# Laying the preparation of a unit out to end one step sooner in each round of a chunked recurrence

## What is computed

```python
def step(S, inp):
    r_t, w_t, k_t, v_t, kk_t, a_t = inp
    sa = jnp.einsum("bhvk,bhk->bhv", S, kk_t)
    S = (S * w_t[:, :, None, :]
         - sa[..., None] * (kk_t * a_t)[:, :, None, :]
         + v_t[..., None] * k_t[:, :, None, :])
    return S, jnp.einsum("bhvk,bhk->bhv", S, r_t)

def rwkv7_readout(o, streams, r_k, gn_g, gn_b, w_out, out_dtype):
    r, v, _, _, _, kd, g = streams
    mean = jnp.mean(o, axis=-1, keepdims=True)
    var = jnp.mean(jnp.square(o - mean), axis=-1, keepdims=True)
    y = ((o - mean) * lax.rsqrt(var + GN_EPS)).reshape(B, T, RW_WIDTH) * gn_g + gn_b
    ...
```

## Time and profile before

| what | value |
|---|---|
| median of 3 runs | 2528.25 us (2522.92 to 2529.23) |
| the profiled execution, its own time | 2539.45 us |
| its span, first to last instruction | 2537.7 us |
| granted TensorE clock, mean | 0.939 of full speed |
| rounds 0 to 20 of the recurrence in it | 562.6 to 1161.4 us, 598.8 us |

### The profile page before, as it was taken

One profiled execution on the slowest core, in us unless ns is written; L12 is line 12 of the kernel. 1 busy time (PEld: TensorE's weight loads), 2 busy tenths in 40 slices (PEclk: granted clock), 3 DMA queues, 4 the chain that ended last, 5 costly groups with the idle time before them and its releaser, 6 DMA issues.

```text
span 2537.7 us, 59405 instructions
## 1 busy us (share of the span) xinstructions
PE 2172.6 (86%) x25764; PEld 1625.2 (64%) x25764; DVE 1354.0 (53%) x2324; ACT 1152.3 (45%) x1933; POOL 681.8 (27%) x412
## 2 busy tenths in 40 slices
PE   8799999288888888887789999996888987898888
PEld 2587777067766767676667666663666665666666
DVE  1357878434444455454345666664356663466752
ACT  2466767233333334343335454543355553355552
POOL 0334443200001011011433222222443332433332
PEclk9899999589998899998989999997999998999998
DMA  7215453652332222312313111111222221222222
GB/s 259 71 59 170 132 159 117 179 147 78 100 105 75 68 63 51 78 43 71 135 56 108 51 50 54 55 42 43 90 75 83 67 67 66 67 79 76 63 67 67
DMA packets 156163, 221.37 MB, mean 87 GB/s; under 512 B 84480, under 2 KB 109312, under 8 KB 155136
## 3 DMA queue, kind: packets, MB, share of 16 engines
q1 hardware_dynamic: 144800, 174.32, 22.4%
q0 software_dynamic: 9952, 40.11, 5.2%
q10 hardware_dynamic: 1152, 3.15, 0.3%
HBM read 164.84 MB, written 42.21 MB: 82 GB/s over the span
## 4 chain that ended last, share of the span: by engine, by line
PE 59%; DVE 15%; ACT 11%; issue 8%; POOL 4%; DMA 2%; SPq 0%; ACTq 0%; DVEq 0%; POOLq 0%
PE ps L257 8%; PE ps L259 7%; PE ps L258 7%; PE ps L1337 3%; PE ps L543 3%; PE ps L1327 2%; PE ps L1352 2%; PE ps L2257 2%; PE ps L396 2%; PE ps L2794 2%; PE ps L2217 1%; PE ps L2771 1%; PE ps L1202 1%; ACT p L2277 1%; DVE s L921 1%
## 5 line engine op out<-in xcount | busy, mean ns | idle before, releaser
L242 POOL TENSOR_TENSOR wbl<-wb,wbh 128x1024 fp32r<-128x1024 f32 x128 | 309.4, 2418 | 661.3 <-ACT wbh L237 657.5
L257 PE MATMUL ps<-hTh,wah 128*128 128x512 f32 (+1 forms) x512 | 180.6, 353 | 17.3 <-POOL wal L242 10.8
L257 PE MATMUL ps<-hT2h,wbh 128*128 128x512 f32 x416 | 180.2, 433 | 10.7 <-POOL wbl L242 10.5
L258 PE MATMUL ps<-hTl,wah 128*128 128x512 f32 (+1 forms) x512 | 174.9, 342 | 0.0
L259 PE MATMUL ps<-hTh,wal 128*128 128x512 f32 (+1 forms) x512 | 174.7, 341 | 0.0
L257 PE MATMUL ps<-hT1h,wbh 128*128 128x512 f32 (+1 forms) x432 | 169.0, 391 | 3.1 <-POOL hT1l L2398 3.1
L344 POOL TENSOR_TENSOR ro<-ro 128x256 f32<-128x256 f32 (+1 forms) x12 | 11.9, 993 | 586.7 <-DVE ro L328 586.7
L237 ACT ACTIVATE wbh<-wb 128x1024 fp32r<-128x1024 f32 x128 | 134.6, 1052 | 69.5 <-PE ps L1936 43.5
L259 PE MATMUL ps<-hT2h,wbl 128*128 128x512 f32 x416 | 164.5, 395 | 0.0
L258 PE MATMUL ps<-hT2l,wbh 128*128 128x512 f32 x416 | 163.9, 394 | 0.0
L242 POOL TENSOR_TENSOR wal<-wa,wah 128x1024 fp32r<-128x1024 f32 x34 | 102.2, 3008 | 219.2 <-ACT wah L237 219.2
(11 more groups left out here) (410 smaller groups left out, 5612.6 us busy)
## 6 DMA issues: line engine op xcount, KB each, us to landing
wb<-in_w_in SPq DMA_DIRECT2D x56, 512.0 KB, 3.5
s_str_dram<-s POOLq DMA_DIRECT2D x48, 576.0 KB, 8.7
wm<-in_ada SPq DMA_DIRECT2D x48, 512.0 KB, 4.5
bkv<-s_str_dram SPq DMA_DIRECT2D x96, 192.0 KB, 3.3
wa<-in_rw_in SPq DMA_DIRECT2D x34, 512.0 KB, 4.4
wb<-in_da_in SPq DMA_DIRECT2D x32, 512.0 KB, 3.4
ARI<-s_str_dram SPq DMA_DIRECT2D x96, 128.0 KB, 3.4
wb<-in_w_out SPq DMA_DIRECT2D x16, 512.0 KB, 3.5
```

The source lines that it names most:

```text
L242: e.tensor_tensor(self.lo[:, n % 2], self.raw[:, n % 3], self.hi[:, n % 2].bitcast(F32), ALU.subtract).then_inc(self.K.s.w_lo, 1)
L257: e.matmul(z, wh[:, k, :], hi[:, k, a:b], start=k == 0, stop=False)
L258: e.matmul(z, wh[:, k, :], lo[:, k, a:b], start=False, stop=False)
```

## The change

The number that `pace` gets for the preparation goes from 7 to 8, and from 11 to 12 in a round with a readout. The generators have seven and eleven steps as before, so the preparation's steps fall due at 1/8, 2/8, ... instead of 1/7, 2/7, ..., with nothing due at the end.

```diff
             if u + 3 < 24:
-                parts.append((prepared(u + 3), 11 if self.read_with(u + 3) else 7))
+
+                parts.append((prepared(u + 3), 12 if self.read_with(u + 3) else 8))
             pace(*parts)
```

## The result

| | before | after |
|---|---|---|
| median | 2528.74 us (2522.92 to 2531.06, 4 runs) | 2557.59 us (2547.14 to 2562.4, 4 runs) |
| ratio | 1 | 1.0104, interval 1.0083 to 1.0126 |
| the profiled execution | 2539.45 us | 2547.14 us |
| its span | 2537.7 us | 2545.3 us |
| its mean granted clock | 0.939 | 0.946 |

The medians are 28.9 us apart. The ratio, which is not the quotient of the two medians, says 1.0%, or 26 us (21 to 32). The forecast was 32.1 us slower and 2560 us.

What follows compares the result with a forecast made beforehand. PE bounds the kernel; its 89 us idle in rounds 0 to 20 are all an order can win back. Terms 7.4 + 2.5 + 28.8 - 3.0 - 3.6 + 0 = +32.1 us on 2528.25 gave 2560 us, range 2541 to 2582.

Steps and rivals of the forecast that it cites:

- the first term: Readout rounds: preparation's L1230 moves ahead of a level, so PE idles before it and before A11's update; 7.4 + 2.5 us slower.
- the second term: Readout rounds: readout's steps move earlier, so DVE's slow root holds back L1495 and the block L1408; 28.8 us slower.
- the third to fifth together: L1202's wait for L1272 shrinks (3.0 us gain), "issue" stops partly covered (3.6 us gain), small shifts in plain rounds (zero).
- the rival that the clock falls once more: New idle times in readout rounds bring one more half-clock stretch each, 18.6 us more, 2579 us; chance 14%.
- the fourth part: "Issue" stops in L1240 move to L1352 at no cost; those in L1337 get L1202's work beneath them, gaining 3.6 us.
- the rival of vanishing stops: PE's "issue" stops in rounds 0 to 20 vanish, 31.1 us less, 2529 us, no difference; chance 10%.
- The milder second term: Readout's chain over ACT, POOL and DVE runs 2 us shorter, six rounds give back 12 us, 2548 us; chance 12%.

Runs made afterwards that it cites:

- only_plain_8: Kernel before with the new number 8 only in the 15 rounds without a readout, readout rounds keeping 11: 2522.98 us, ratio 0.9964.
- plain_8_tail_later: Kernel before with 8 in rounds without a readout, and DVE's L350, L1652 and L1654 of a readout put off to the next round: 2499.83 us, ratio 0.9872.
- root_only: Kernel before, but in the six readout rounds only the readout's steps stand earlier, as in the change: 2551.91 us, ratio 1.0081.
- plain_7_tail_later: Kernel before with its numbers 7 and 11, only DVE's L350, L1652 and L1654 of a readout put off to the next round: 2505.26 us, ratio 0.9891.

## Why the prediction was right, and where its sum was not

**The direction, the place and the total held.** The waits forecast for the changed profile came out row for row: L1230 waits 1.81 us (1.9 forecast), A11's L1352 1.06 us (0.9), L1608 1.99 us (2), L1408 4.60 us in round 12 (5), L1363 at most 1.1 us (1), and L1202 no longer for L1272. The time, 2557.59 us, is 2.4 us below 2560.

**The lengths of the rounds did not come out, and one sign of being wrong did.** The prediction expected 5 to 7 us more in each readout round, the same length within a microsecond elsewhere, and called itself wrong if rounds without a readout shortened by a microsecond or more each. From the profile of before to that of after the six readout rounds grow by 5.8 to 9.2 us each, 48.8 us together, and the fifteen others shrink by 36.3 us, 2.4 us each: 24.9 us in the five that follow a readout round, 11.4 us in the other ten. The timed runs of only_plain_8 put the plain rounds' own part of this at 9 us, 0.6 us each. The second profile of the change has the same pattern, 51.0 us more and 26.9 us less. The premise that fails with it is the prediction's first: that PE's idle time is all that an order can win or lose. Between the two stretches PE's idle time grew by 25.6 us, to 114.6, while its busy time fell by 12.9 us, from 509.75 to 496.82. In plain_8_tail_later the stretch is 36.4 us shorter than before, and 18.9 us of that are busy time:

```profile
560.00:1122.40 562.40, 490.83 (x16047) 407.22 (x16048) 274.95 (x453) 235.09 (x376) 43.22 (x38) 0.96 0.28 77
```

**The terms are less good than their sum.** The parts alone measure +14 us for the first (9.9 forecast), +20.5 us for the second (28.8) and -9 us for the third to fifth together (-6.6). They add up to 25.8 us, against 25.6 us for the whole in its second comparison; the forecast sum, 32.1, is 6 us too high, and lies at the very end of the first comparison's interval (21 to 32 us). That the time came within 2.4 us of the forecast is in part luck: the first term was too low by 4.5 us, the second and the rest too high by 8 and 2.5 us. One reading was off too: round 6 was given round 12's 11.08 us from L1352 to L1363, and its own rows have 761.69 - 749.33 = 12.36 us, which takes 1.3 us from the second term.

**The step that failed is the one that took the clock for neutral in the second term.** I priced the stretch from the update L1352 to L1363 at 15.3 us. In the profile of after it is 939.55 - 921.88 = 17.67 us in round 12. L1608 waits 1.99 us and is granted a clock of 0.52, so that it takes 927.25 - 924.51 = 2.74 us to L1400's start in place of 1.49 us; the block, from L1408 to L1363, takes 5.04 us in place of 3.86 us (in all six readout rounds, 4.9 to 5.3 us). These rows of after have L1608 in the first, DVE's wait in the second, the block in the third and the 6.2 us behind L1363 in the fourth.

```profile
924.50:927.30 2.80, 2.79 (x8) 1.11 (x8) 0.00 (x0) 0.00 (x0) 0.00 (x0) 0.52 0.00 0
929.90:934.50 4.60, 0.02 (x3) 0.00 (x0) 3.34 (x4) 0.60 (x1) 2.62 (x3) 1.00 0.00 0
934.50:939.50 5.00, 4.43 (x160) 4.11 (x160) 2.87 (x5) 0.62 (x2) 2.62 (x2) 0.66 0.70 169
939.50:945.70 6.20, 6.06 (x134) 5.10 (x138) 1.48 (x2) 4.26 (x6) 1.59 (x2) 1.00 0.97 261
```

In exchange the next round starts fast. This is the granted clock of the 6.2 us behind the L1363 that ends each readout round:

| round | 6 | 8 | 12 | 14 | 18 | 20 |
|---|---|---|---|---|---|---|
| before | 0.50 | 0.52 | 0.50 | 0.72 | 0.72 | 0.50 |
| after | 1.00 | 0.72 | 1.00 | 1.00 | 1.00 | 0.97 |
| root_only | 1.00 | 1.00 | 1.00 | 1.00 | 1.00 | 0.95 |
| plain_7_tail_later | 0.73 | 1.00 | 1.00 | 1.00 | 1.00 | 1.00 |

Before, the long wait stood at the very end of the round, with the next round's first steps behind it at the lower level. Now the slow time comes earlier, over the block and in some rounds over L1608; only part of it, 11 of 44 us in the six rounds, falls where PE is idle. The run that has the second term alone shows what this is worth. In root_only's profile, an execution at its median, the six readout rounds are 39.0 us longer than before, 10 us more than the 28.8 us, and the five plain rounds behind are 20.5 us shorter, where the prediction had nothing. The two together are 18.5 us, near the 20.5 us that the timed runs give. So the step that failed is this term's size, 28.8 us for 20.5, for want of the clock on both sides of L1363. It rests on single executions for its two halves, and on timed runs for their sum. Of the rival that the clock falls once more, one half happened (L1608 and the block are slowed) and the other half was the reverse of what I priced.

The Trainium skill ("TensorE: Matmul & The Clock Gate", section "HAM oscillation — how this bites in real kernels") tells of waits that leave the work behind them at half rate, and the rows before and after agree. The rows also show that it matters which work stands behind the wait.

**The first term** was priced by its waits alone too, and measures 14 us (10 to 19) for waits that are there to a tenth. Its six new idle times of 1.8 us come with the old L1363 wait still in place; whether the clock makes the rest, the runs do not show.

**The stops by "issue"** moved with the count of instructions, as the fourth part said, from L1240 and L1337 into L1352, and did not vanish: the four largest rows are 34.7 us before, 30.8 us after and 39.9 us with only the plain rounds changed. So the rival of vanishing stops is refuted, and the gain of 3.6 us is not shown. How much of the plain rounds' 9 us comes from the stops and how much from L1202's wait for L1272, no run separates.

**The milder second term** as I put it, a shorter chain from L1608 to the last L350, is not what happened: that distance is 933.32 - 924.51 = 8.8 us after in round 12, and 7.56 us before. The extra is L1608 at low clock; in rounds 8 and 18, where L1608 ran at full clock, the block began 8.71 us behind L1608, as forecast (8.85).

## What to carry to other kernels

When one number shifts a whole stage against others, ask it of each kind of round apart: here the same edit gains 9 us in fifteen rounds and costs 33 us in six. Before moving a step that hands data between several engines (here a reciprocal root over ACT, DVE and POOL, 7.6 us), look at what comes behind it in each engine's line, since a slow exchange blocks whatever is next, and moving it as a whole only chooses the victim. Splitting it, so that the part that waits comes one round later in a hole of the engine, took 28 us off the kernel, where moving it whole, one step earlier, cost 20 us. And before a cause is named by taking it away from the changed kernel, take it away from the kernel before as well: the tail that cost 18 us in the one cost 28 us in the other.

## What the hardware showed that I had not expected

- Taking the longest part of a wait off PE's line before dense work is worth more than its length here. In plain_7_tail_later L1363's waits, 2.4 and 4.3 us before in rounds 14 and 12, are down by 15.3 us in all, and the time by 28 us (21 to 34). The profiles show where most of the rest is: the 6.2 us behind the six L1363 were granted 0.50 to 0.72 before and, but for one at 0.73, 1.00 then (table above). By 6.2 us times what the clock lacks of 1.00, an estimate, 15.7 us were lost there before and 1.7 us then. The timed runs of plain_7_tail_later have mean clocks from 0.943 to 0.949, those of before beside them 0.936 to 0.943. That nothing else is in it is not shown by a run of its own.
- Executions of one and the same kernel differ by 1% along with their mean granted clock: 2519.67 us at 0.946 and 2546.18 us at 0.936 for the kernel before. A single profiled execution, however closely read, did not give the size of this change: 7.7 us between the two profiles, 28.9 us between the medians.
- PE stops with no wait in sight for 2 us and up to 6.4 us at once behind dense code of 64x64 matmuls. The traces tie this to the instruction queue. All 15 such stops over 1 us in the stretch before end 1.3 to 1.5 us behind the end of a 16 KB packet of that queue, and so do all 10 after (1.3 to 1.6 us), though only one such packet comes in each 4.7 us of the stretch. The Trainium skill ("Runtime: NRT & Kernel Launch", section "Instruction fetch mechanics") calls the cost of a block's boundary mostly hidden; here it was not. No run took the fetch away.
